# Two-layer hybrid trunk with a routed MoE: the router's choice by max and index, counts moved behind the first gate product, one gather split

## The reference

```python
def hier_moe(h, w_grp, b_grp, w_exp, b_exp, w_gate, w_up, w_down):
    xt = h.reshape(T, D)                                   # T = 256, D = 1024
    grp_logits = xt @ w_grp + b_grp                        # 4 groups
    grp_prob = softmax(grp_logits)
    g_idx = argmax(grp_logits); g_w = grp_prob[tok, g_idx]
    exp_logits = (xt @ w_exp + b_exp).reshape(T, 4, 8)     # 8 experts in a group
    top_l, top_j = top_k(exp_logits[tok, g_idx], 2)
    wts = softmax(top_l) * g_w[:, None]
    e_idx = g_idx[:, None] * 8 + top_j
    # every token goes through its two experts of 32, each
    #   (silu(x @ w_gate[e]) * (x @ w_up[e])) @ w_down[e]     1024 -> 512 -> 1024
    # and the two results are added with the weights wts
```

## Time and profile before

| | |
|---|---|
| median of 3 runs | 1158.44 us (1155.75 to 1160.93) |
| the profiled execution | 1157.77 us, its span (first to last instruction) 1156.0 us |
| mean granted TensorE clock | 0.904 of 2.4 GHz |
| HBM read | 440.01 MB, 382 GB/s over the span |
| busy share | PE 76%, PEld 56%, DVE 26%, ACT 16%, POOL 2% |

### The profile page before, as it was taken

One profiled execution on the slowest core, in us unless ns is written; L12 is line 12 of the kernel. 1 busy time (PEld: TensorE's weight loads), 2 busy tenths in 40 slices (PEclk: granted clock), 3 DMA queues, 4 the chain that ended last, 5 costly groups with the idle time before them and its releaser, 6 DMA issues.

```text
span 1156.0 us, 28729 instructions
## 1 busy us (share of the span) xinstructions
PE 877.0 (76%) x12822; PEld 645.5 (56%) x12822; DVE 302.3 (26%) x956; ACT 186.9 (16%) x494; POOL 24.9 (2%) x28
## 2 busy tenths in 40 slices
PE   7999998788575757575779999788585756566776
PEld 6765647576363636464556446676464535455454
DVE  3476735122010101111104674222111101111101
ACT  4223532111000000000003442011000000000000
POOL 1121000000000000000000000000000000000000
PEclk9999999899898988888889999899878888888788
DMA  9955347999999999999999966999999999999997
GB/s 378 427 202 217 145 145 283 427 418 426 430 429 428 428 429 429 428 428 429 428 424 424 381 239 244 376 427 420 429 428 429 428 429 429 427 428 431 427 424 295
DMA packets 33979, 441.93 MB, mean 382 GB/s; under 512 B 3840, under 2 KB 4992, under 8 KB 7296
## 3 DMA queue, kind: packets, MB, share of 16 engines
q1 hardware_dynamic: 33632, 440.92, 91.2%
q10 hardware_dynamic: 288, 0.15, 0.0%
HBM read 440.01 MB, written 1.05 MB: 382 GB/s over the span
## 4 chain that ended last, share of the span: by engine, by line
DMA 55%; PE 34%; DVE 5%; ACT 3%; issue 2%; SPq 1%; DVEq 0%; ACTq 0%
DMA side<-weights 45%; DMA ring<-weights 10%; PE PS L512 8%; PE PS L957 8%; PE PS L940 6%; PE PS L668 1%; PE PS L833 1%; PE PS L522 1%; PE PS L559 1%; DVE scr L1515 1%; DVE side L1748 1%; ACT side L1304 1%; SPq L331 1%; PE PS L597 1%; PE PS L849 1%
## 5 line engine op out<-in xcount | busy, mean ns | idle before, releaser
L940 PE MATMUL PS<-ring,probT 128*32 128x128 f32 x4480 | 151.4, 296 | 62.2 <-DMA ring<-weights 58.9
L940 PEld LDWEIGHTS PS<-ring,probT 128*32 128x32 f32 x4480 | 135.3, 119 | 77.1 <-DMA ring<-weights 68.3
L940 PE MATMUL PS<-side,probT 128*32 128x128 f32 x2688 | 106.4, 324 | 66.9 <-DMA side<-weights 65.0
L940 PEld LDWEIGHTS PS<-side,probT 128*32 128x32 f32 x2688 | 92.9, 131 | 87.3 <-DMA side<-weights 81.7
L512 PE MATMUL PS<-ring,side 128*128 128x512 f32 (+1 forms) x320 | 137.1, 580 | 0.5 <-DMA ring<-weights 0.5
L1515 DVE TENSOR_TENSOR scr<-scr,PS 128x128 f32<-128x128 f32 x64 | 18.4, 288 | 393.4 <-ACT scr L1419 331.7
L512 PEld LDWEIGHTS PS<-ring,side 128*128 128x128 f32 x320 | 59.5, 192 | 63.4 <-issue 61.9
L2018 DVE COPY probT<-PS 32x256 f32<-32x256 f32 x112 | 47.5, 424 | 168.6 <-PE PS L957 167.8
L957 PE MATMUL PS<-side,scr 128*32 128x256 f32 x864 | 69.0, 467 | 24.9 <-DMA side<-weights 21.2
L957 PE MATMUL PS<-ring,scr 128*32 128x256 f32 x896 | 67.0, 449 | 19.5 <-DVE scr L2014 10.0
L1423 ACT ACTIVATE probT<-PS 32x256 f32<-32x256 f32 x112 | 41.8, 373 | 229.1 <-PE PS L957 228.4
(11 more groups left out here) (275 smaller groups left out, 824.6 us busy)
## 6 DMA issues: line engine op xcount, KB each, us to landing
ring<-weights SPq DMA_DIRECT2D x126, 2048.0 KB, 34.1
side<-weights SPq DMA_DIRECT2D x76, 2048.0 KB, 27.1
side<-weights SPq DMA_DIRECT2D x8, 512.0 KB, 24.8
ring<-weights SPq DMA_DIRECT2D x4, 512.0 KB, 8.8
xn<-weights SPq DMA_DIRECT2D x2, 1024.0 KB, 5.8
side<-weights SPq DMA_DIRECT2D x2, 1024.0 KB, 10.7
ring<-weights SPq DMA_DIRECT2D x2, 1024.0 KB, 28.5
xn<-xT_in SPq DMA_DIRECT2D x2, 512.0 KB, 5.5
```

The lines of the kernel that those rows point to most:

```text
L940: mm = pe.matmul(PS[f * CAP:(f + 1) * CAP, b, up * P:(up + 1) * P], gatherT[:, k, tok], w[:, k, f * P:(f + 1) * P], start=(k == 0), stop=( ...
```

## The change

`choose` finds the group with `dve.max` and `dve.max_index` over eight values (four group logits and four constants of -1e30, which GpSimd writes once), compares the group index with a table of each expert's group, and gets both experts' masks in one comparison of 64 columns; they are added for `m`. Ten instructions stand there in place of eleven. `first_picks` compares the rank in PSUM plus one with the places at once and multiplies by the mask times `rs`, which is made (`mrs`) before the ranks are there; the masked rank in SBUF, which the later quads need, is written behind it by `keep_rank`. The counts are two products of ones behind the first gate product, with a semaphore `counted` of their own. Of the gather of t = 0 two products of eight now follow the rank product of t = 1. The table grows by 32 columns.

```diff
-            def gather_half(half, t):
-                for k in range(4):
-                    d = 4 * half + k
+            def gather_part(t, ds):
+                for d in ds:
+                    half, k = d // 4, d % 4
                     mm = pe.matmul(PS[:, half, k * P:(k + 1) * P], x[:, t, d * P:(d + 1) * P], pick[:, t, :],
...
-                pe.matmul(PS[:, 7, 32:64], tb("ones"), m[:, 0, :], start=True, stop=False, skip_group_check=True)
-                pe.matmul(PS[:, 7, 64:96], tb("ones"), m[:, 0, :], start=False, stop=False, skip_group_check=True)
+                pe.matmul(PS[:, 7, 32:64], tb("ones"), m[:, 0, :], start=True, stop=False)
                 pe.wait_ge(first_picked, layer + 1)
-                for half in range(2):
-                    gather_half(half, 0)
+                gather_part(0, range(6))
                 pe.wait_ge(chosen, 2 * layer + 2)
-                pe.matmul(PS[:, 7, 32:64], tb("tri"), m[:, 1, :], start=False, stop=True, skip_group_check=True)
-                pe.matmul(PS[:, 7, 64:96], tb("ones"), m[:, 1, :], start=False, stop=True,
-                          skip_group_check=True).then_inc(ranked, 1)
+                pe.matmul(PS[:, 7, 32:64], tb("tri"), m[:, 1, :], start=False, stop=True).then_inc(ranked, 1)
+                gather_part(0, range(6, KD))
...
                         mm.then_inc(chunk_done, 1)
+                        if first and e == 0 and up == 0:
+                            for t in range(TT):
+                                mm = pe.matmul(PS[:, 7, 64:96], tb("ones"), rt[:, 0, t, :], start=(t == 0),
+                                               stop=(t == 1))
+                            mm.then_inc(counted, 1)
...
-                link(dve.scalar_tensor_tensor(lg[:, t, :], PS[:, 4 if t else 6, t * 64:t * 64 + NR],
-                                              s("rs")[:, t:t + 1], rb, ALU.mult, ALU.add))
-                lgrp = lg[:, t, 0:N_GRP]
-                link(dve.tensor_reduce(gm, lgrp, AX.X, ALU.max))
-                link(dve.scalar_tensor_tensor(gk, lgrp, gm, rev[:, 0:N_GRP], ALU.is_equal, ALU.mult))
-                link(dve.tensor_reduce(km, gk, AX.X, ALU.max))
-                link(dve.tensor_scalar(gk, gk, km, NEG, ALU.not_equal, ALU.mult))
-                link(tt(lm.rearrange("p (g e) -> p g e", g=N_GRP),
-                        lg[:, t, N_GRP:NR].rearrange("p (g e) -> p g e", g=N_GRP),
-                        last(gk, N_EXP // N_GRP), ALU.add))
+                link(dve.scalar_tensor_tensor(g8[:, 0:N_GRP], logits[:, 0:N_GRP], rs, rb[:, 0:N_GRP], ALU.mult, ALU.add))
+                dve.max(gtop, g8)
+                link(dve.scalar_tensor_tensor(lg[:, t, 0:N_EXP], logits[:, N_GRP:NR], rs, rb[:, N_GRP:NR],
+                                              ALU.mult, ALU.add))
+                link(dve.max_index(gat, gtop, g8))
+                link(tt(lm, gat[:, 0:1].broadcast_to([P, N_EXP]), tb("gid").bitcast(U32), ALU.not_equal))
+                link(dve.scalar_tensor_tensor(lm, lm, NEG, lg[:, t, 0:N_EXP], ALU.mult, ALU.add))
                 link(dve.max(top, lm))
                 link(dve.max_index(at, top, lm))
-                link(dve.tensor_scalar(idx, at[:, 0:2], -1.0, 64.0, ALU.mult, ALU.add))
-                link(dve.tensor_scalar(o1, rev, idx[:, 0:1], None, ALU.is_equal))
-                dve.scalar_tensor_tensor(m, rev, idx[:, 1:2], o1, ALU.is_equal, ALU.add).then_inc(chosen, 1)
+                link(tt(rt[:, 3:5, t, :], last(at[:, 0:2], N_EXP), mid(tb("ids").bitcast(U32), 2), ALU.is_equal))
+                tt(m, rt[:, 3, t, :], rt[:, 4, t, :], ALU.add).then_inc(chosen, 1)
...
                 add_quarter(layer, 1, first_chunk, iters)
+                dve.wait_ge(chosen, 2 * layer + 1)
                 first_picks(layer, 0, None).then_inc(first_picked, 1)
                 evacuate_last(layer, 1)
+                keep_rank(0)
...
                 first_picks(layer, 1, build).then_inc(m_onehot, 1)
-
-                tt(rt[:, 4, :, :], rt[:, 0, :, :], rt[:, 3, :, :], ALU.subtract)
+                keep_rank(1)
...
+                mrs = s("mrs")[:, QE * t:QE * (t + 1)]
+                dve.tensor_scalar(mrs, rt[:, 0, t, 0:QE], s("rs")[:, t:t + 1], None, ALU.mult)
                 dve.wait_ge(ranked, 2 * layer + t + 1)
-                link(dve.scalar_tensor_tensor(rank[:, t, :], PS[:, 7 if t else 5, t * 32:(t + 1) * 32], 1.0,
-                                              rt[:, 0, t, :], ALU.add, ALU.mult))
-                raw = tt(pickw[:, t, :].rearrange("p (e c) -> p e c", e=QE), last(rank[:, t, 0:QE], CAP),
-                         mid(tb("iota"), QE), ALU.is_equal)
+                raw = pickw[:, t, :].rearrange("p (e c) -> p e c", e=QE)
+                ins = dve.scalar_tensor_tensor(raw, last(ranks(t)[:, 0:QE], CAP), 1.0, mid(tb("iota"), QE),
+                                               ALU.add, ALU.is_equal)
...
-                return dve.tensor_scalar(pick[:, t, :], pickw[:, t, :], s("rs")[:, t:t + 1], None, ALU.mult)
+                return tt(pick[:, t, :].rearrange("p (e c) -> p e c", e=QE), raw, last(mrs, CAP), ALU.mult)
+
+            def keep_rank(t):
+                link(dve.scalar_tensor_tensor(rank[:, t, :], ranks(t), 1.0, rt[:, 0, t, :], ALU.add, ALU.mult))
...
+                dve.wait_ge(counted, layer + 1)
                 link(dve.tensor_reduce(s("cmx"), PS[:, 7, 64:96], AX.X, ALU.max))
```

38 lines of the change are left out of this document (24 added, 14 removed), and 4 rows, old and new, of the table ident.

## The result

Changed kernel: median 1149.39 us over 11 runs (1147.32 to 1159.19); the kernel before, beside it on the same chip, 1155.57 over 11 (1153.56 to 1160.93). The ratio is 0.9950, 95% interval 0.9933 to 0.9966: 5.8 us faster (3.9 to 7.7), where 1.05 were forecast. The profiled execution took 1147.94 us; the one before took 1157.77.

The account below looks back on a forecast made before the run. Bytes at 428 GB/s bound the kernel except at two places per MoE where DMA queues run short. Reaching the later place 0.84 + 0.21 = 1.05 us earlier took 1158.44 to 1157.4 us, range 1154.0 to 1161.0.

Parts of the forecast that it names:

- The chain: Router work from choice through rank product, picks and second-half gather to gate product; first loads issued 1.28 and 0.65 us earlier.
- Choice of t = 1: VectorE's expert choice for the second half of the tokens, second router: 2.41 us in place of 2.71.
- Rank product: TensorE's product giving the ranks, now without the count product of 0.24 us: 0.41 us in the second router.
- picks up to the gather: From the ranks to the gather of t = 1: 0.81 us with two linked instructions, 0.18 less than before.
- the comparison from PSUM: First instruction of the new picks, 128x128: taken as 0.35 us, between bounds of 0.29 and 0.48.
- The integer comparisons: In the choice, without a measured row: 0.19 us as plain ones, each possibly 0.06 more.
- Counts: Two count products between gate and up of the first expert: 0.44 us added to TensorE's chain a router.
- The gain in starting: Gather of t = 1, and so each MoE's first load behind the gate product, 1.28 and 0.65 us earlier.
- The second place: Load waiting for the second quad's second-expert down product; queue runs short there, limiting the gain to 0.84 + 0.21 us.
- its first rival: The late load's wait in each MoE doesn't bind; the full 1.93 us counts, giving 1156.5 us; chance 0.2.
- The clock: TensorE, standing still about 1 us in the second router, falls to half clock more often: 1158.9 us; chance 0.15.
- one spell less: One stretch of TensorE at half clock fewer than before, in a router or its first quads: 1155.8 us.

Follow-up runs that it names:

- e1: Kernel before with only the table 32 unused columns and `st` 48 columns wider, so later buffers lie as in the changed kernel: 1151.90 us, ratio 0.9971.
- e6: Changed kernel with 32 more columns of zeros in the table, putting `side`'s start back at 236 modulo 256 bytes: 1150.26 us, ratio to before 0.9948.
- e13: Kernel before with six unread products a router, two ahead of the rank product of t = 1 and four behind it: 1153.77 us, ratio 0.9977.
- e4: Changed kernel with SP's loop issuing the next quad's first load ahead of the load waiting for the previous quad's down product: 1145.84 us, ratio to before 0.9920.
- e3: Changed kernel with all eight gather products of t = 0 ahead of the rank product again: 1148.95 us, ratio to before 0.9946.
- e2: Changed kernel with the count products back in their old places: 1152.47 us, ratio to before 0.9961.
- e12: Kernel before with only the count products moved behind the first gate product: 1155.66 us, ratio 0.9998.
- e7: Changed kernel with the old picks (masked rank, comparison, scaling) and no `keep_rank`: 1147.09 us, ratio to before 0.9922.
- e16: Changed kernel with e4's load order and the count products in TensorE's waits, in a PSUM bank of their own: 1146.39 us, ratio to before 0.9917.

## Why the prediction was wrong

**The step that failed** is the sentence "GpSimd's extra write and 32 columns of the table lie in the first microseconds, far from any wait". As a count of time it was right; but the columns also move `side`'s four buffers, into which more than a third of 440 MB is loaded, from 236 to 108 modulo 256 bytes. Shown: with nothing but the wider table and `st` the steady rate is 431 and not 428 GB/s and the time 3.4 us less, 1.3 to 5.5 (e1); moved back, the rate and the time behind the late loads are back (e6), though the timed runs of e6 are too noisy to show it. The forecast's premise, that 262 to 560 us runs by bytes alone and no engine changes it, held; that the bytes' own rate was a constant was never asked. Of all steps it was the only one that reached 828 us and not 20.

**The chain.** Term by term the sum nearly held. Choice of t = 1: 710.57 to 712.88, 2.31 us (2.41 forecast). Rank product 0.42 (0.41), picks up to the gather 714.05 - 713.35 = 0.70 (0.81), the comparison from PSUM 0.29 where 0.35 was taken. The integer comparisons took 0.19 on 32 columns and 0.22 on 64, no dearer than the float ones. Counts 0.56 a router where 0.44 was taken from the old rows: that was 0.12 too cheap each time. The floor of about 25 ns a matmul, of the Trainium skill, page "TensorE: Matmul & The Clock Gate", section "Wait — 56ns, not 53.3ns?", with its estimate of 0.10, was further off still. The gain in starting was larger than forecast: routed to first load fell by 9.39 - 7.78 = 1.61 and 10.28 - 7.88 = 2.40 where 1.28 and 0.65 stood. In the first router at full clock it is 8.58 - 7.78 = 0.8 (e13's against the changed kernel's); the rest is the clock.

**The second place** binds, as the forecast and not its first rival had it: the loss there grew by 0.6 and 1.3 us, and where the load behind it was freed (e4) it vanished.

**The clock** was a rival with the wrong sign. I feared that TensorE, standing still for 1 us in one piece, would fall to half clock more often. Its waits ahead of and behind the rank product went from 0.55 + 1.01 = 1.56 to 0.95 + 0.18 = 1.13 us; the second, which I had not counted, shrank most, and the late spells went from 5 of 8 to 0 of 22. The prediction did price "one spell less", at 1155.8. It goes with the result, and e13 supports it from the other side, in one router of two; how much of the 5.8 us it makes is not settled, since a spell's place is partly chance.

**The sum, afterwards.** The rate gives 3.4 to 4.1 us (3.4 timed in e1, 3.8 behind the late loads of the profiles of before and after, 4.1 in the mean of all), and the router with its clock, less what the second place takes back, the other 2 or so of the 5.8 measured: e1 stands at 0.9971 and the changed kernel at 0.9950. This split is as uncertain as the intervals are wide. Neither split, nor counts, nor picks shows by itself (e3, e2 and e12, e7). The base was also drawn badly: the median of three runs, 1158.44, lay above the 1155.5 to 1157.2 of the longer series. From 1155.57 the same steps would have given about 1154.5 before the rate; still 5 us above what was measured.

**A better version.** e4's turned loop, alone or with the counts in the waits, is the best that was found: 1145.84 us at a ratio of 0.9920, and 1146.39 at 0.9917 (e16).

## What to carry to other kernels

In a kernel that runs at the speed of its loads, look at what a change does to the addresses of the buffers loaded into, above all one that only adds a few columns to a table; and measure the move by itself, a kernel with nothing but the padding, before crediting the edit: here the padding alone gave 3.4 of the 5.8 us. When a wait is shortened, look for the next place at which the same queue runs dry, since it takes back what the first gives; turning the order of two loads there was worth 1.7 to 2.6 us by the profiles, where the shorter router at full clock is worth 0.8 in each MoE. Count all the gaps of TensorE in a stretch, and not the one that grows, before saying which way its clock will go.

## What the runs showed of the hardware

- The rate from HBM into SBUF went with where four of the eleven buffers, and what lies ahead of them behind the table, start within 256 bytes: 428 to 429 GB/s at 236 and 0, 430 to 431 at 108 and 128, in twenty profiles over some 300 us each.
- A router can be shorter with more products in it: e13's six useless ones a router made the kernel 2.7 us faster (0.8 to 4.6), in line with one wait less of 1.01 us and no late spell in its two routers.
- An early spell of half clock, on work behind which TensorE waits anyway, cost 0.2 to 0.4 us with the new choice; a late one, on the path, 1.5 to 1.7.
- The index search on eight values took 0.16 us and the maximum 0.17, against 0.18 and 0.20 on 32 columns: over this range the width hardly counts.
